# Order of the parts of the inner width in both FFNs: 12, 16, 16 tiles in place of 16, 16, 12

## Chip, core and metric

The kernel runs on one core of one Trainium2 chip. The metric is the device time of one execution in microseconds (us), here the median of three runs. One execution of the kernel before was also taken with the hardware profiler; all rows below are of that one.

## What is computed

Two transformer blocks on one sequence of 256 tokens with 2048 channels, in fp32. Each ends with an FFN of inner width 5632, that is 44 tiles of 128 channels. The first has a causal depthwise convolution of 3 taps between up-projection and gate:

```python
def conv_glu_ffn(h, w_up, cw, cb, w_down):
    u = causal_depthwise_conv(h @ w_up, cw, cb)
    a, gate = jnp.split(u, 2, axis=-1)
    return (jax.nn.silu(gate) * a) @ w_down
```

and the second is `x + (silu(h2 @ w_gate) * (h2 @ w_up)) @ w_down`. After the first FFN come the final norm of block 1 and the input norm of block 2; after the second comes the last norm and the output.

## The kernel before

**Layout.** Channels lie on the 128 partitions, tokens along the free axis (T = 256). x holds 16 tiles. Every weight is split on the chip into a high part (ScalarE, `hi`, L544, the copy itself is L550) and a low part (VectorE, `lo`, L888, the subtraction is L893), both in w_two; activations are likewise split and lie as high and low halves (512 columns) in hp and yp. For each weight tile TensorE runs a pair of matmuls (`unit` L1601): high weight on 512 columns (L1612) and low weight on 256 (L1613).

**Units and slots.** Weights come in units of k tiles by 256 output columns, through R = 4 slots of w_raw and w_two. SyncE issues two DMAs for each unit (L413) as soon as the low part of the slot's earlier unit is done. `hi` of a unit waits until TensorE has used the unit four before it, `lo` waits for `hi`, TensorE for `lo`.

**Phases.** PHASES (L76) lists all weight phases: name, units in a step, steps, output chunks in a step. Each engine has its own program that goes through the phases in this order, written by hand; counters of semaphores are worked out from the table. A part of k tiles of the FFN's inner width gives two phases: up{b}_{p}, k/2 steps of 8 units of 4 tiles, and down{b}_{p}, 4 steps of 8 units of k/4 tiles (a step makes 512 output channels, as two groups of 4 units). So a part of 16 tiles has down units of 4 tiles, one of 12 tiles units of 3 tiles, and `unit_words` (L377) tells both splitting engines how wide a unit is. Each step of an up phase makes two tiles of the gated inner width, called mid; the last of them are finished behind the last matmul of the up phase:

- block 1 (`conv_step`, L736 and L1302): VectorE adds the two halves of the sum out of PSUM (L909, called take), scales (L1010), ScalarE and VectorE do the taps (L731, L1295), ScalarE the sigmoid (L721), VectorE two products (L1317, L1318), ScalarE the high part of mid (L748), VectorE its low part (L1323);
- block 2 (`work`, L1335): the same without taps, low part at L1341.

TensorE's `gemm` (L1634) runs a down phase. Its unit u waits for this many tile pairs of mid:

```python
gemm(f"down{blk}_{p}", m, n, lambda u: (sem("mid"), done + -(-(u + 1) * (n // 4) // 2)))
```

that is 2, 4, 6, 8 of 8 pairs with 16 tiles and 2, 3, 5, 6 of 6 with 12: the fourth unit needs the last pair in both.

**Closing phases.** The parts are added into x on VectorE (`residual`, L1264, with adds at L1268 and L1269). The last part (p == 2, tests at L756 and L1349) isn't a plain stream but `closing` (L601 on ScalarE, L948 on VectorE): while its steps run, the finished tiles of x are squared (L594; with the final gain too at the end of block 1, L597), multiplied by the next norm's gain (L599) and split (L945), with GpSimd adding the squares up (L879). w_out and w_out_2 close in the same way, each with 4 steps; w_out_2 has units of 4 tiles. In the next phase TensorE runs `stats` (L1671): 1-column matmuls that sum squares over channels (L1684), eight for each kind and pair of tiles, behind the next phase's first unit (`opening`, L1696). At the end of block 1 (k == 3) there are two kinds of squares, elsewhere one. In down2_2, which ends the program, `early` (L1656) puts three turns of output (L1588) and the first stats ahead of the very last unit.

Of the kernel before, what the change touches and what calls it, by code (L numbers as in the profile page):

```python
# [47 lines left out]
GC = 256  # L48
# [19 lines left out]
for _name, _cols in (("ident", P), ("flip", P), ("rot", P), ("ones", P), ("cos", T), ("sin", T),  # L68
# [2 lines left out]
    _n += _cols  # L71
NCST = _n

PARTS = [(0, 16), (16, 16), (32, 12)]

PHASES = [("conv", 32, 1, 16), ("kv", 24, 1, 12), ("gates", 2, 1, 1), ("q", 16, 1, 8), ("w_out_conv", 16, 1, 16),  # L76
          ("w_out", 4, 4, 4)]
for _p, (_t, _k) in enumerate(PARTS):
    PHASES += [(f"up1_{_p}", 8, _k // 2, 4), (f"down1_{_p}", 8, 4, 4)]
PHASES += [("latent", 8, 2, 4), ("latent_last", 4, 1, 2), ("kpe", 2, 1, 1), ("mla", 8, 8, 9), ("mla_proj", 8, 4, 4),  # L80
           ("diff", 16, 8, 8), ("diff_proj", 8, 4, 4), ("w_out_2", 8, 4, 4)]
for _p, (_t, _k) in enumerate(PARTS):
    PHASES += [(f"up2_{_p}", 8, _k // 2, 4), (f"down2_{_p}", 8, 4, 4)]
# [47 lines left out]
class Chain:  # L131
# [6 lines left out]
    def link(self, ins):  # L138
        ins.then_inc(self.sem, 1)
        self.k += 1  # L140
        self.wait()
# [59 lines left out]
def program(nc, A, cst_d, out):  # L201
# [5 lines left out]
    with ctx:  # L207
# [169 lines left out]
        def unit_words(ph, j):  # L377
            if ph == "mla" and j < 2:
                return 3 * 384
            return 3 * GC if ph in ("down1_2", "down2_2") else 4 * GC  # L380

        FIRST = {n: m for (n, *_), (m, *_) in zip(PHASES, PHASES[1:])}

# [17 lines left out]
        def _(sp):  # L401
# [75 lines left out]
            def ffn(blk, wa, ca0, wg, cg0, wd):  # L477
                for p, (t0, n) in enumerate(PARTS):
                    ph = f"up{blk}_{p}"
                    with sp.Fori(0, STEPS[ph]) as i:  # L480
                        for g, (w, c) in enumerate(((wa, ca0), (wg, cg0))):
                            col = sp.snap(i * GC + (c + t0 * P))
                            for u in range(4):
                                halves(ph, i, 4 * g + u, w, 4 * u, 4, col)
                    gemm(f"down{blk}_{p}", wd, t0, n, 0)
# [47 lines left out]
        def _(act):  # L533
# [10 lines left out]
            def hi(ph, i, j):  # L544

                s, r = slot_of(ph, j)
                n = unit_words(ph, j)
                act.wait_ge(raw_ready[s], arrived(ph, i, j))
                act.wait_ge(unit_used, i * UPS[ph] + (U0[ph] + j + 1 - R + LEAD))
                nc.scalar.activation(w_hi[:, s, 0:n], w_raw[:, s, 0:n], ACT.Copy).then_inc(hi_ready, 1)  # L550
# [163 lines left out]
            def ffn(blk):  # L714
                for p, (t0, n) in enumerate(PARTS):
                    up = f"up{blk}_{p}"
# [136 lines left out]
        @block.gpsimd  # L853
        def _(pool):
            for s in range(R):
                nc.gpsimd.memset(small[:, 60 + s:61 + s], 0.0).then_inc(lo_ready[s], 1)


            for ph in ("conv", "kv", "gates", "q"):
                for j in range(3 if ph == "conv" else 0, UPS[ph]):  # L860
                    if ph == "conv" and j == 7:
                        pool.wait_ge(sem("bias_row"), 1)
                        pool.dma_start(bias_d, bias_row[0:NQ, :]).then_inc(sem("bias_stored"), 16)
                    if ph == "conv" and j == 10:
                        pool.wait_ge(sem("bias_stored"), 16)
                        pool.dma_start(bias_win, bass.AP(bias_d.tensor, 0, [[1, P], [3 * P, NQ], [1, T]])).then_inc(loaded["bias"], 16)
                    s = slot_of(ph, j)[0]
                    n = unit_words(ph, j)
                    pool.wait_ge(hi_ready, U0[ph] + j + 1)
                    nc.gpsimd.tensor_tensor(w_lo[:, s, 0:n], w_raw[:, s, 0:n], w_hi[:, s, 0:n].bitcast(f32), ALU.subtract)\  # L870
                        .then_inc(lo_ready[s], 1)

            for k in (1, 3, 4, 5):
                for p in range(1, KT // 2 - 1):
                    for src, name, done, nth in ((sq, "squares", "summed", NTH[k]), (sq_g, "squares_g", "summed_g", 0))[:2 if k == 3 else 1]:
                        pool.wait_ge(sem(name), KT // 2 * (nth + 1) + p + 1 if nth or name == "squares" else 2 * p + 2)
                        if p > 1:
                            pool.wait_ge(sem(done), (KT // 2 - 2) * nth + p - 1)
                        nc.gpsimd.tensor_tensor(src[:, 0:2, :], src[:, 0:2, :], src[:, 2 * p:2 * p + 2, :], ALU.add).then_inc(sem(done), 1)  # L879
# [3 lines left out]
        def _(dve):  # L883
# [4 lines left out]
            def lo(ph, i, j):  # L888

                s, r = slot_of(ph, j)  # L890
                n = unit_words(ph, j)
                dve.wait_ge(hi_ready, i * UPS[ph] + (U0[ph] + j + 1))
                v.tensor_tensor(w_lo[:, s, 0:n], w_raw[:, s, 0:n], w_hi[:, s, 0:n].bitcast(f32), ALU.subtract)\  # L893
                    .then_inc(lo_ready[s], 1)
# [380 lines left out]
            def ffn(blk):  # L1275
                if blk == 1:
                    v.memset(ua[:, :, 0:FTAPS - 1], 0.0)
                    link(v.memset(ug[:, :, 0:FTAPS - 1], 0.0))
                for p, (t0, n) in enumerate(PARTS):
                    up, down = f"up{blk}_{p}", f"down{blk}_{p}"  # L1280
# [302 lines left out]
        def _(pe):  # L1583
# [50 lines left out]
            def gemm(ph, rhs, ktiles, operand, between={}):  # L1634

                nu = UPS[ph] // 2
                ku = ktiles // nu
                k = CLOSING.get(ph)

                def step(i, hooks={}):  # L1640
                    for g in range(2):
                        free(ph, i, -2 + 2 * g)
                        for u in range(nu):
                            if (g, u) in hooks:
                                hooks[g, u]()
                            unit(ph, i, nu * g + u, u * ku, ku, GC, (2 * g, 2 * g + 1), rhs, ktiles - 1, operand(u))

                if between:
                    step(0, between)
                whole = STEPS[ph] - (k is not None)  # L1650
                with pe.Fori(1 if between else 0, whole) as i:
                    step(i)
                if k is not None:
                    step(whole, {(1, nu - 1): lambda: early(k)})
# [41 lines left out]
            def opening(k, at):  # L1696

                return {(0, 1): lambda: stats(k, (0, 1, KT - 2, KT - 1)), at: lambda: spread(k)}
# [36 lines left out]
            def normed(k):  # L1735
                if k == 0:
                    return lambda u: (sem("normed_lo"), 2 * u + 2)
                return lambda u: (sem("gained_lo"), KT * NTH[k] + 4 * u + 4)
# [161 lines left out]
            def ffn(blk, k):  # L1900
                h, m = (hp, yp) if blk == 1 else (yp, hp)
                for p, (t0, n) in enumerate(PARTS):
                    gemm(f"up{blk}_{p}", h, KT, normed(k), opening(k, (0, 3)) if p == 0 else {})
# [169 lines left out]
```

## Time and profile before

| | us |
|---|---|
| median of 3 runs | 2911.27 |
| lowest and highest | 2909.68 and 2912.64 |
| the profiled execution, its own time | 2908.53 |
| its span, first to last instruction | 2906.7 |
| TensorE busy in the span | 2852.2 (98%) |
| VectorE, ScalarE, GpSimd busy | 2089.7, 1378.8, 218.8 |
| mean granted TensorE clock | 0.989 |

The span lies inside the time of the same execution; the difference, 1.8 us, is what lies around it. Matmuls are pipelined, so the listed durations of neighbours overlap, and the step from one start to the next is the pace. PEclk is the granted clock as a share of full speed.

### The profile page before, as it was taken

To read this page: it belongs to the slowest core of one execution; us is meant where nothing else is said; L and a number is where in the kernel's file an instruction comes from. 1 tells how busy PE (TensorE), PEld (TensorE's weight loads), DVE (VectorE), ACT (ScalarE), POOL (GpSimd) and SP (SyncE) were. 2 spreads that over 40 slices of the span, in tenths; PEclk is the share of its full clock that TensorE was granted. 3 is DMA by queue.
4 is the path that set the end of the run, shared out by engine and by line. 5 is a ranking of instruction groups with operands and counts; after the bars stand their busy time and mean duration, and the time that the engine had idled before them with its cause. 6 is when DMAs were issued, how large, how long until landed. Compare 5 with 4: busy or idle time off the path is not lost.

```text
span 2906.7 us, 49543 instructions
## 1 busy us (share of the span) xinstructions
PE 2852.2 (98%) x16793; PEld 2489.9 (86%) x16793; DVE 2089.7 (72%) x3289; ACT 1378.8 (47%) x1807; POOL 218.8 (8%) x111
## 2 busy tenths in 40 slices
PE   7998999999999999999999999999999999999998
PEld 6887888888888888888888888888888888888887
DVE  4976777876886687777866777777667766775675
ACT  4324655643554455545443455544455433433434
POOL 4865010000000001100000000000000000000001
PEclk9999999999999999999999999999999999999999
DMA  9645356665655665655555555555555556565654
GB/s 238 181 135 130 95 138 185 185 193 181 187 185 191 185 190 167 178 139 151 153 172 183 169 175 165 179 166 188 185 181 184 189 195 191 176 201 189 188 170 148
DMA packets 605082, 507.34 MB, mean 175 GB/s; under 512 B 90156, under 2 KB 603068, under 8 KB 604604
## 3 DMA queue, kind: packets, MB, share of 16 engines
q1 hardware_dynamic: 604347, 504.00, 57.3%
q0 software_dynamic: 560, 2.12, 0.2%
q8 instruction: 53, 0.87, 0.1%
q14 instruction: 42, 0.34, 0.0%
q10 hardware_dynamic: 80, 0.01, 0.0%
HBM read 503.88 MB, written 2.12 MB: 174 GB/s over the span
## 4 chain that ended last, share of the span: by engine, by line
PE 91%; DVE 4%; ACT 2%; SPq 1%; issue 0%; DMA 0%; POOL 0%; DVEq 0%; ACTq 0%
PE banks L1612 54%; PE banks L1613 28%; PE banks L1625 3%; PE banks L1627 1%; PE banks L1588 1%; ACT hp_f L669 1%; DVE w_two L893 1%; DVE banks L1085 1%; PE banks L1703 0%; PE banks L1958 0%; ACT w_two L550 0%; DVE arena L909 0%; PE banks L2007 0%; PE banks L1684 0%; SPq L397 0%
## 5 line engine op out<-in xcount | busy, mean ns | idle before, releaser
L550 ACT ACTIVATE w_two<-w_raw 128x1024 fp32r<-128x1024 f32 (+2 forms) x960 | 996.8, 1045 | 1161.9 <-PE banks L1613 1073.3
L1612 PE MATMUL banks<-hp,w_two 128*128 128x512 f32 x4160 | 1475.5, 399 | 9.5 <-POOL w_two L870 6.5
L893 DVE TENSOR_TENSOR w_two<-w_raw,w_two 128x1024 fp32r<-128x1024 f32 (+2 forms) x889 | 1071.6, 1217 | 533.1 <-ACT w_two L550 515.6
L1613 PE MATMUL banks<-hp,w_two 128*128 128x256 f32 x4160 | 1167.0, 281 | 0.0
L1612 PE MATMUL banks<-yp,w_two 128*128 128x512 f32 x2752 | 963.8, 395 | 3.9 <-DVE yp L1323 2.6
L1612 PEld LDWEIGHTS banks<-hp,w_two 128*128 128x128 f32 x4160 | 784.7, 189 | 197.8 <-issue 10.3
L1613 PEld LDWEIGHTS banks<-hp,w_two 128*128 128x128 f32 x4160 | 789.3, 190 | 1.4 <-issue 1.0
L1613 PE MATMUL banks<-yp,w_two 128*128 128x256 f32 x2752 | 771.8, 280 | 0.0
L1612 PEld LDWEIGHTS banks<-yp,w_two 128*128 128x128 f32 x2752 | 516.9, 188 | 123.3 <-DVE yp L1323 3.6
L1613 PEld LDWEIGHTS banks<-yp,w_two 128*128 128x128 f32 x2752 | 521.2, 189 | 0.1
L909 DVE TENSOR_REDUCE arena<-banks 128x256 f32<-128x512 f32 (+1 forms) x392 | 251.4, 683 | 80.2 <-PE banks L1613 73.1
L879 POOL TENSOR_TENSOR arena<-arena 128x512 f32<-128x512 f32 x30 | 45.6, 1527 | 2569.5 <-ACT arena L594 2569.5
L870 POOL TENSOR_TENSOR w_two<-w_raw,w_two 128x1024 fp32r<-128x1024 f32 x71 | 171.1, 2423 | 98.3 <-ACT w_two L550 98.3
L1085 DVE SCALAR_TENSOR_TENSOR banks<-arena,vec,banks 128x256 f32<-128x256 f32 x232 | 102.0, 485 | 3.7
L1625 PE MATMUL banks<-w_two,hp 128*128 128x512 f32 x256 | 92.6, 404 | 0.0
L1295 DVE SCALAR_TENSOR_TENSOR arena<-arena,vec 128x256 f32<-128x256 f32 x176 | 77.5, 482 | 17.2 <-ACT arena L731 11.3
L1010 DVE TENSOR_TENSOR arena<-arena,cst 128x512 f32<-128x512 f32 x120 | 82.9, 691 | 3.9
L1612 PE MATMUL banks<-arena_r,w_two 128*128 128x512 f32 x208 | 77.5, 411 | 0.0
L731 ACT ACTIVATE arena<-arena,vec 128x256 f32<-128x256 f32 x88 | 48.2, 595 | 51.3 <-DVE arena L1010 51.3
L1627 PE MATMUL banks<-w_two,hp 128*128 128x256 f32 x256 | 71.9, 281 | 0.0
L721 ACT ACTIVATE arena<-arena 128x512 f32<-128x512 f32 x44 | 27.8, 633 | 80.6 <-DVE arena L1010 61.4
L1268 DVE TENSOR_TENSOR x<-banks,x 128x256 f32<-128x256 f32 (+1 forms) x128 | 53.1, 415 | 15.9 <-PE banks L1613 15.9
(265 smaller groups left out, 1750.4 us busy)
## 6 DMA issues: line engine op xcount, KB each, us to landing
w_raw<-in_w_in SPq DMA_DIRECT2D x480, 256.0 KB, 3.1
w_raw<-in_w_up SPq DMA_DIRECT2D x352, 256.0 KB, 2.9
w_raw<-in_w_ffn_up SPq DMA_DIRECT2D x176, 256.0 KB, 3.7
w_raw<-in_w_ffn_gate SPq DMA_DIRECT2D x176, 256.0 KB, 3.0
w_raw<-in_w_down SPq DMA_DIRECT2D x160, 256.0 KB, 3.0
w_raw<-in_w_ffn_down SPq DMA_DIRECT2D x160, 256.0 KB, 3.0
w_raw<-in_w_out SPq DMA_DIRECT2D x128, 256.0 KB, 3.1
w_raw<-in_w_mla_proj SPq DMA_DIRECT2D x64, 256.0 KB, 3.0
```

The costliest lines, as they stand in the source:

```text
L550: nc.scalar.activation(w_hi[:, s, 0:n], w_raw[:, s, 0:n], ACT.Copy).then_inc(hi_ready, 1)
L870: nc.gpsimd.tensor_tensor(w_lo[:, s, 0:n], w_raw[:, s, 0:n], w_hi[:, s, 0:n].bitcast(f32), ALU.subtract)\
L893: v.tensor_tensor(w_lo[:, s, 0:n], w_raw[:, s, 0:n], w_hi[:, s, 0:n].bitcast(f32), ALU.subtract)\
L909: v.tensor_reduce(dst, pair(b)[0:rows], X, ALU.add).then_inc(chunk_out, 1)
L1010: return v.tensor_tensor(dst, dst, bcast(r_row, 2), ALU.mult)
L1085: ins = v.scalar_tensor_tensor(conv_y[:, t, :] if k == TAPS - 1 else acc, src, w, acc, ALU.mult, ALU.add)
L1268: link(v.tensor_tensor(xt, banks[:, c, 0:T], xt, ALU.add))
L1295: ins = v.scalar_tensor_tensor(dst[:, c, :], buf[:, c, k:k + T], vdyn("ffn_conv_w", at_ch[c] + k * 2 * FT), dst[:, c, :], ALU.mult, ALU.add)
L1612: mm(banks[:, b, :], w_hi[:, s, at:at + P], rhs[:, kt, :], start=kt == kt_first, stop=False)
L1613: ins = mm(banks[:, b, 0:T], w_lo[:, s, at:at + P], rhs[:, kt, 0:T], start=False, stop=kt == kt_last)
L1625: mm(banks[:, b, :].rearrange("p (a n) -> p a n", a=2), rhs[:, kt, b * P:(b + 1) * P], w_two[:, :, s, at], start=kt == 0, stop=False)
L1627: ins = mm(banks[:, b, 0:T], rhs[:, kt, T + b * P:T + (b + 1) * P], w_hi[:, s, at], start=False, stop=kt == kt_last)
```

## The change

The 44 tiles are cut into parts of 12, 16 and 16 tiles. Thereby up{b}_0 has 6 steps and up{b}_2 has 8; down{b}_0 has units of 3 tiles and down{b}_2 of 4. `unit_words` follows. Which phase closes, and all else, is untouched.

```diff
-PARTS = [(0, 16), (16, 16), (32, 12)]
+PARTS = [(0, 12), (12, 16), (28, 16)]
...
         def unit_words(ph, j):
             if ph == "mla" and j < 2:
                 return 3 * 384
-            return 3 * GC if ph in ("down1_2", "down2_2") else 4 * GC
+            return 3 * GC if ph in ("down1_0", "down2_0") else 4 * GC
```

## Rows read from the trace of the kernel before

**Rows 1.** The page: span and busy time of each engine.

```profile
span 2906.7 us, 49543 instructions
...
PE 2852.2 (98%) x16793; PEld 2489.9 (86%) x16793; DVE 2089.7 (72%) x3289; ACT 1378.8 (47%) x1807; POOL 218.8 (8%) x111
```

**Rows 2.** TensorE's waits, whole span: total us, times, longest us.

```profile
PE banks L1684 <- ACT arena L594: 5.0, 3, 2.4
...
PE banks L1612 <- DVE yp L1323: 2.6, 2, 2.3
...
PE banks L1612 <- DVE hp L1341: 1.0, 1, 1.0
```

**Rows 3.** Timeline, TensorE in down1_2: start us, us, instruction; 42 such starts.

```profile
1159.62 0.39 PE L1612 MATMUL banks<-yp,w_two 128*128 128x512 f32 x1
...
1173.83 0.40 PE L1612 MATMUL banks<-yp,w_two 128*128 128x512 f32 x1
```

**Rows 4.** Splits of units of 4 and 3 tiles: busy, mean ns, idle before.

```profile
L550 ACT ACTIVATE w_two<-w_raw 128x1024 fp32r<-128x1024 f32 x880 | 925.8, 1058 | 1106.1 <-PE banks L1613 1018.9 <-PE banks L1627 45.4 <-DMA w_raw<-in_w_in 25.9
L550 ACT ACTIVATE w_two<-w_raw 128x768 fp32r<-128x768 f32 x64 | 53.2, 842 | 52.5 <-PE banks L1613 51.1 <-DMA w_raw<-in_w_ffn_down 1.3
...
L893 DVE TENSOR_TENSOR w_two<-w_raw,w_two 128x1024 fp32r<-128x1024 f32 x809 | 985.9, 1229 | 491.3 <-ACT w_two L550 474.0 <-DVE hp L1341 7.8 <-DVE arena L1492 1.5
...
L893 DVE TENSOR_TENSOR w_two<-w_raw,w_two 128x768 fp32r<-128x768 f32 x64 | 64.7, 1028 | 38.0 <-ACT w_two L550 37.9
```

**Rows 5.** Chain that ended last: the ends of up1_0, up1_2 and up2_2.

```profile
617.30 1.30 DVE arena L909 x2
...
625.10 0.70 DVE yp L1323
...
1111.42 1.30 DVE arena L909 x2
...
1119.21 0.70 DVE yp L1323
...
2823.00 1.21 DVE arena L909 x2
...
2827.54 0.70 DVE hp L1341
```

**Rows 6.** Timeline at the end of down1_2: VectorE, ScalarE, TensorE.

```profile
1181.20 2.52 DVE L893 TENSOR_TENSOR w_two<-w_raw,w_two 128x1024 fp32r<-128x1024 f32 x2 [2.12 <-ACT w_two L550]
...
1184.44 0.41 DVE L1268 TENSOR_TENSOR x<-banks,x 128x256 f32<-128x256 f32 x1
...
1180.13 3.00 ACT L550 ACTIVATE w_two<-w_raw 128x1024 fp32r<-128x1024 f32 x3
1186.13 0.63 ACT L594 ACTIVATE arena<-x 128x512 f32<-128x512 f32 x1 [3.01 <-DVE x L1269]
...
1184.72 1.03 PE L1684 MATMUL banks<-cst,arena 128*128 128x1 f32 x8
1186.81 4.29 PE L1684 MATMUL banks<-cst,arena 128*128 128x1 f32 x24 [1.06 <-ACT arena L594]
```

**Rows 7.** The same at the end of w_out_2.

```profile
2153.24 0.42 DVE L1268 TENSOR_TENSOR x<-banks,x 128x256 f32<-128x256 f32 x1
...
2154.94 0.63 ACT L594 ACTIVATE arena<-x 128x512 f32<-128x512 f32 x1 [0.83 <-DVE x L1269]
...
2155.76 1.93 PE L1684 MATMUL banks<-cst,arena 128*128 128x1 f32 x16
```

**Rows 8.** ScalarE's squares with the final gain: busy, mean ns.

```profile
L597 ACT ACTIVATE arena<-x,vec 128x256 f32<-128x256 f32 x16 | 7.9, 494 | 0.0
```

**Rows 9.** TensorE at the end of w_out.

```profile
439.38 1.05 PE L1684 MATMUL banks<-cst,arena 128*128 128x1 f32 x8 [1.46 <-ACT arena L594]
```

**Rows 10.** Stretches: us, busy of PE, PEld, DVE, ACT, POOL, PEclk, DMA share, GB/s.

```profile
436.00:446.00 10.00, 8.54 (x48) 7.60 (x47) 6.92 (x18) 4.88 (x7) 0.00 (x0) 0.83 0.58 168
1116.00:1123.00 7.00, 4.66 (x19) 3.83 (x18) 5.17 (x8) 3.46 (x5) 0.00 (x0) 0.76 0.24 69
1184.00:1195.00 11.00, 9.94 (x52) 9.19 (x51) 7.06 (x27) 4.86 (x9) 0.00 (x0) 0.69 0.46 142
2152.00:2162.00 10.00, 10.00 (x65) 8.99 (x64) 7.58 (x19) 7.39 (x9) 0.00 (x0) 1.00 0.45 145
2824.00:2832.00 8.00, 7.02 (x41) 5.91 (x40) 6.44 (x10) 3.79 (x5) 0.00 (x0) 1.00 0.31 96
```

## The prediction

> **What bounds the kernel.** I read the page first: TensorE is busy for 2852.2 of 2906.7 us [rows 1], and no other engine is near that. So the change pays or costs only through what TensorE waits for, or the clock it is granted. Next the list of TensorE's waits [rows 2]: of all of them three kinds touch FFN parts. At L1612 it waits 2.6 us in two places for the last mid of block 1, one of 2.3, so the other is 0.3. It waits 1.0 for the last mid of block 2. At L1684 it waits 5.0 in three places for squares behind a closing phase, 2.4 the longest. The reader should see that all of this is 8.6 us, and that the up and down loops themselves show no wait.
>
> **Pace.** In down1_2 42 listed starts of L1612 lie between 1159.62 and 1173.83 [rows 3]: 14.21 / 41 = 0.3466 us for one weight tile (a pair of matmuls). A unit of 4 tiles is 8 pairs, 2.77 us; one of 3 tiles is 6 pairs, 2.08 us. In both kinds the splitting engines are quicker: 1.058 and 1.229 us for 4 tiles, 0.842 and 1.028 for 3 [rows 4]. The short ones' idle time before ScalarE's copies is 52.5 us, of which 51.1 ended with TensorE and 1.3 with a DMA: the loads are in time at the short pace too.
>
> **What the change moves, part by part.**
>
> *Work.* Each block keeps one part of 12 and two of 16: 22 up steps, 12 down steps, 32 short down units and 64 long ones. Matmuls, splits, bytes, DMA issues (two for each unit on SP) and residual adds are the same in number and size, only in another order; GpSimd's adds too. 0 us. The short units' loads, issued on SP, now come ahead of up1_1 and up2_1 instead of the closing. They are hidden by the four slots, as the 1.3 us above shows; without that cover each late load would cost TensorE directly, and the bound is those 1.3 us. The first units of the following up phase are ready at the latest one copy and one subtraction (1.06 + 1.23 = 2.3 us) after the last short unit frees a slot, and three of them (8.3 us) run before the fourth is wanted. 0 us.
>
> *The wait for the last mid.* It moves with the short part. From the take to the low part's end it is 8.50 us at the end of up1_0 (617.30 to 625.10 + 0.70) and 8.49 at that of up1_2 (1111.42 to 1119.21 + 0.70) [rows 5]: the chain doesn't depend on which part it is. TensorE covers it with three down units, 8.32 us for long and 6.24 for short ones. The differences, 0.2 and 2.2, are the measured 0.3 and 2.3. After the change down1_0 waits 0.3 + 2.08 = 2.4 and down1_2 about 2.3 - 2.08 = 0.2: 2.6 together, as before, so 0.0. In block 2 the chain is shorter (2823.00 to 2827.54 + 0.70 = 5.2, after a split that is late [rows 5]); the 1.0 of down2_2 goes to down2_0 and down2_2's falls to 0: 0.0. Bounds: 0.3 either way, the difference between the two block 1 chains as they meet the cover.
>
> *The wait for squares at the end of block 1.* This is where something changes. VectorE should take the last residual as soon as the last down unit ends. In the list of its instructions [rows 6] it waits 2.12 us for ScalarE's splits, does two (2.52 us) and starts the residual at 1184.44. The last down unit ended one unit of 2.77 before the stats at 1184.72 (some 0.1 between), at about 1181.8: the residual is 2.6 us late. ScalarE was late with these splits because the previous pair's squares and gains held it until 1180.13. Four short units (8.3 us) are too little for this round trip between two engines. The square comes at 1186.13, and TensorE has stood for 1.06 us before the 24 stats at 1186.81. w_out_2 closes with long units (11.1 us for four) and is the model for down1_2 after the change [rows 7]: stats at 2155.76, so the last unit ended near 2152.8 and the residual at 2153.24 is only 0.4 late; the square starts at 2154.94, ends at 2155.6, and the 16 stats run with no wait. Down1_2 has two more squares to a pair there (L597, 0.494 each [rows 8]), that is some 1.0 us more on ScalarE before the splits; with 11.1 - 8.3 = 2.8 us more room that still fits. So the 1.06 goes: **-1.1 us**, bounds 0 (ScalarE as late as now) and -1.1. Nothing else is late next: eight stats (1.03 us [rows 6]) run before the squares of the last pair are wanted.
>
> *The end of the program.* The 2.4 us of [rows 2] there is the run from the last matmul through four adds and a square; it starts when the last unit ends, whatever its size. The last unit gets 0.7 us longer, one among others that are shorter. 0 us; there are three turns and eight stats before it, and they have more room now. Also 0.
>
> *The clock.* TensorE runs at 2.4 GHz nearly always. In five stretches [rows 10] it is seen what a wait does. At the end of w_out, with a wait of 1.46 among stats [rows 9], the granted clock is 0.83 over 10 us: 10 x 0.17 = 1.7 us of full speed missing. Around the 2.3 us wait in down1_2 it is 0.76 over 7, again 1.7. At the end of down1_2, where 32 one-column matmuls and the 1.06 wait lie together, 0.69 over 11: 3.4 us missing. At the end of w_out_2 (16 such matmuls, no wait) and around the 1.0 wait of down2_2 it is 1.00: nothing. So a fall to 1.2 GHz costs in pieces of 1.7. The fall around the mid wait moves to down1_0 with the same wait: 0, with -1.7 to +1.7 as bounds. At the end of block 1 the wait goes but the 32 one-column matmuls stay, about 4.1 us of them at 1.03 for eight: nearer to w_out (16 of them and a wait, 3.5 us in all, a fall) than to w_out_2 (1.93 us, none). I take the fall as staying, 0 us, with -3.4 as the other bound.
>
> The Trainium skill (TensorE: Matmul & The Clock Gate, section "The HAM clock gate") says that the full clock is released by activity and that the hardware's look at it is free-running, not tied to the kernel. By that rule the same wait in another place may be met by a fall or not, so it speaks against carrying the falls over one to one, and the sum would be anything from -1.1 - 5.1 = -6.2 to -1.1 + 3.4 = +2.3 us.
>
> **Sum.** 0 + 0.0 - 1.1 + 0 + 0 = -1.1 us. Against the profiled execution's 2908.53 that is 2907.4. That execution lies 2.7 below the median of 2911.27 and 1.2 below the lowest run, so I put the difference on the median: **2910.2 us**.
>
> **Rivals.**
>
> *A, forecast (0.40):* wait gone, falls as before. 2910.2.
>
> *B, the fall at the end of block 1 goes too (0.25).* For it: w_out_2's end at 1.00. Against: twice as many one-column matmuls in a row. It gives 3.4 less the part that was spent standing (1.06 x 0.5 = 0.5), so -1.1 - 2.9 = -4.0: 2907.3. Half of it (one piece of 1.7) lies between A and B.
>
> *C, slower (0.17):* the fall takes hold in the fourth unit of down2_0's first step. There the 1.0 us wait stands alone at 1.00 now; at its new place it may be met by a fall. One piece costs 1.7, two 3.4: -1.1 + 1.7 = +0.6 to -1.1 + 3.4 = +2.3, so about 2912.7. It decides from a fall of over 1.1 us on. Against it: at the same wait nothing fell. (The clock gate page of the Trainium skill, by the section named above, leaves this open.)
>
> *D, nothing to measure anywhere (0.10):* the change doesn't bring what the steps say, because ScalarE with its extra squares is as late as before. 2911.3. For it: the two extra squares. Against it: 2.8 us more room.
>
> *E, faster by over 0.2% (0.04):* that is 5.8 us, about what a measurement of this kernel can tell from no change. It takes the wait, both falls in block 1 (5.1) and some more, as the wait of 2.3 in down1_0 being covered. -6.2 to -8: 2904.2. Every wait of the five places with both falls is 8.6 + 5.1, so more can't come.
>
> *F, slower by over 0.2% (0.04):* something in every step, as late loads or splits, at 0.2 us in each of the 44 up steps of both blocks: 8.8 - 1.1 = +7.7. No row shows such a wait. 2919.0.
>
> **How the numbers follow.** A, B, C and D lie between 2907.3 and 2913.6. With the runs' own spread of 1.5 about the median and the bounds of 0.3 and 1.3 for mid and loads, 2905.3 to 2914.3 leaves out E and F and the tails of B and C. All but E and F are within 5.8 us, so same has 0.90 with the rest of the tails shared: faster 0.06, same 0.89, slower 0.05.
>
> **What the changed profile would show.** TensorE's waits: at L1612 for L1323 again 2.6 in two places, the long one near 580 us instead of 1117 (up1_0 has two steps of 8 x 2.77 us less, so it ends 44 us before 617); for L1341 1.0, now near 2294 (six such steps and three short units behind 2155) instead of 2828; at L1684 two places with 3.9 instead of three with 5.0. The residual at the end of down1_2 starts within 0.5 us of the last matmul, and the 24 stats have no idle before them. TensorE's busy time stays at 2852 give or take 3. Wrong would be: a long wait at down1_2's mid still (the chain is what matters there, not the cover), a wait before 24 stats, or a new wait in up1_1 or up2_1 behind the short units.

## Result, and the profile after

| | before | after |
|---|---|---|
| median of 20 runs, us | 2910.09 | 2917.59 |
| lowest and highest | 2899.86, 2912.99 | 2905.76, 2924.19 |
| ratio, 95% interval | | 1.0024, 1.0016 to 1.0031 |
| the profiled execution | 2908.53 | 2907.34 |
| its span | 2906.7 | 2905.6 |

The change makes the kernel slower by 7.5 us in the median, a little over what can be told from no change. The profiled execution alone says otherwise: it is 1.2 us faster than the one of before, and is the second fastest of its 20. One profile of each kernel, compared by its span, would have led to the wrong sign. What follows explains both. The mean granted clock of every timed execution in this document is 0.987 to 0.994, except for one of e8_before_restart (4214.64 us at 0.619), which is left out of that run's median.

Nearly all that the steps foretold of waits is there. TensorE's waits in the profiled execution of the changed kernel (in all us, times, longest):

```profile
PE banks L1684 <- ACT arena L594: 3.9, 2, 2.4
...
PE banks L1612 <- DVE yp L1323: 2.9, 3, 2.3
...
PE banks L1612 <- DVE hp L1341: 1.0, 1, 1.0
```

The wait at L1341 is still 1.0 [rows 2], L1684 is down from three waits and 5.0 to two and 3.9, and L1323's long one is still 2.3. L1323 has three waits, though, where two and 2.6 in all were foretold: one of 0.3 is new, at 823, at the end of up1_1. In the kernel before, a weight load was 0.4 late there for L1323 too, without a wait of a matmul. The end of down1_2 in three timelines, VectorE, ScalarE, TensorE:

```profile
1167.88 2.70 DVE L893 TENSOR_TENSOR w_two<-w_raw,w_two 128x1024 fp32r<-128x1024 f32 x2 [2.12 <-ACT w_two L550]
...
1171.29 0.42 DVE L1268 TENSOR_TENSOR x<-banks,x 128x256 f32<-128x256 f32 x1
...
1172.99 0.63 ACT L594 ACTIVATE arena<-x 128x512 f32<-128x512 f32 x1 [0.89 <-DVE x L1269]
...
1173.68 4.83 PE L1684 MATMUL banks<-cst,arena 128*128 128x1 f32 x32
```

In [rows 6] the residual was 2.6 us late. Now, by the same working, it is some 0.5 late (the last unit ended one unit of 2.77 and some 0.1 before the stats at 1173.68, at about 1170.8), and all 32 one-column matmuls run without idle. The granted clock still falls there, as forecast: 0.73 over 11 us against 0.69 in [rows 10]. Around the long mid wait, now near 577, it doesn't fall at all (1.00 over 574 to 584, where [rows 10] had 0.76). The view of stretches of the changed kernel, columns as in [rows 10]:

```profile
574.00:584.00 10.00, 7.66 (x45) 6.47 (x44) 8.06 (x12) 5.17 (x7) 0.00 (x0) 1.00 0.45 136
1171.00:1182.00 11.00, 11.00 (x61) 10.22 (x60) 6.51 (x24) 5.92 (x10) 0.00 (x0) 0.73 0.45 138
2280.00:2288.00 8.00, 7.01 (x40) 5.91 (x40) 6.50 (x10) 3.79 (x5) 0.00 (x0) 1.00 0.25 76
640.00:880.00 240.00, 239.74 (x1384) 209.40 (x1383) 185.28 (x246) 116.10 (x135) 0.00 (x0) 1.00 0.61 190
2340.00:2540.00 200.00, 200.00 (x1133) 173.33 (x1132) 138.88 (x160) 79.68 (x80) 0.00 (x0) 1.00 0.59 186
2560.00:2800.00 240.00, 240.00 (x1360) 208.15 (x1359) 157.52 (x183) 93.07 (x92) 0.00 (x0) 1.00 0.59 186
```

**What the steps had not asked.** The last three rows above are stretches of steady up and down work at full clock, with no wait but the 0.3 in the first. The number in brackets is how many matmuls TensorE did. The view of stretches of the kernel before, for the same three and one more of block 1:

```profile
640.00:880.00 240.00, 240.00 (x1361) 208.25 (x1360) 178.27 (x235) 111.72 (x128) 0.00 (x0) 1.00 0.59 185
910.00:1090.00 180.00, 180.00 (x1040) 158.69 (x1039) 129.80 (x170) 81.78 (x92) 0.00 (x0) 1.00 0.61 189
2340.00:2540.00 200.00, 200.00 (x1156) 176.34 (x1155) 130.72 (x155) 78.46 (x77) 0.00 (x0) 1.00 0.59 189
2560.00:2800.00 240.00, 240.00 (x1387) 211.59 (x1386) 159.08 (x186) 95.41 (x94) 0.00 (x0) 1.00 0.59 188
```

In 2560 to 2800 TensorE did 1387 matmuls before and 1360 after, in the same time, at PEclk 1.00, never idle. 240 us / (1387 / 2) is 346 ns for a pair, 240 / (1360 / 2) is 353 ns. Block 1 has it the other way round: in 640 to 880 before had 1361 and after has 1384. So the stream of matmul pairs has two paces, 2% apart. The slow one begins right behind the moved wait. The timeline of TensorE in down2_0 of the changed kernel (start, length, instruction, idle before it):

```profile
2282.37 0.39 PE L1612 MATMUL banks<-hp,w_two 128*128 128x512 f32 x1
...
2282.72 0.39 PE L1612 MATMUL banks<-hp,w_two 128*128 128x512 f32 x1
...
2283.06 0.39 PE L1612 MATMUL banks<-hp,w_two 128*128 128x512 f32 x1
...
2284.56 0.50 PE L1612 MATMUL banks<-hp,w_two 128*128 128x512 f32 x1 [0.99 <-DVE hp L1341]
...
2285.01 0.40 PE L1612 MATMUL banks<-hp,w_two 128*128 128x512 f32 x1
...
2285.38 0.40 PE L1612 MATMUL banks<-hp,w_two 128*128 128x512 f32 x1
...
2285.72 0.40 PE L1612 MATMUL banks<-hp,w_two 128*128 128x512 f32 x1
...
2286.07 0.40 PE L1612 MATMUL banks<-hp,w_two 128*128 128x512 f32 x1
```

Ahead of the wait the starts of L1612 are 0.69 apart for two (2282.37, 2282.72, 2283.06), the quick pace within the rounding of the rows. Behind it the starts are 2285.01, 2285.38, 2285.72, 2286.07: 1.06 for three, 353 ns each, and the rows list 0.40 us where they listed 0.39. It stays so to the last norm's stats at 2887. Before, block 2's only wait for a mid was at 2827, some 60 us ahead of those stats.

A simple measure shows it in every profile: the time from one norm's stats (L1674, the matmul ahead of them) to the next. Block 1's FFN lies between the stats after w_out and those after down1_2, block 2's between those after w_out_2 and the early ones of the last norm. Block 2's two in TensorE's timeline, before and then after:

```profile
2155.62 0.28 PE L1674 MATMUL banks<-small,cst 128*128 128x4 f32 x2
...
2889.06 0.28 PE L1674 MATMUL banks<-small,cst 128*128 128x4 f32 x2
```

```profile
2144.37 0.28 PE L1674 MATMUL banks<-small,cst 128*128 128x4 f32 x2
...
2887.35 0.28 PE L1674 MATMUL banks<-small,cst 128*128 128x4 f32 x2
```

Before: 1184.58 - 436.75 = 747.8 and 2889.06 - 2155.62 = 733.4. After, in the profiled execution: 739.9 and 743.0. Block 2 lost 9.6 us. Block 1 gained 7.9, most of it because it ran at the quick pace in this execution; the repeat below shows that it needn't.

### The profile page after: what moved, and what is told of

It is laid out like the page before. It is cut to its first block, busy times and chain, and to the rows that moved or that the text cites. A ratio compares the mean times of both kernels' runs of the same rounds, so it can differ in the third digit from the quotient of the medians.

```text
span 2905.6 us, 49539 instructions
## 1 busy us (share of the span) xinstructions
PE 2849.6 (98%) x16793; PEld 2480.2 (85%) x16793; DVE 2087.7 (72%) x3289; ACT 1368.8 (47%) x1799; POOL 220.5 (8%) x111
## 4 chain that ended last, share of the span: by engine, by line
PE 92%; DVE 4%; ACT 2%; SPq 1%; issue 0%; DMA 0%; POOL 0%; DVEq 0%; ACTq 0%
PE banks L1612 55%; PE banks L1613 27%; PE banks L1625 3%; PE banks L1627 1%; PE banks L1588 1%; ACT hp_f L669 1%; DVE w_two L893 1%; DVE banks L1085 1%; PE banks L1703 0%; PE banks L1958 0%; DVE arena L909 0%; PE banks L2007 0%; SPq L397 0%; PE banks L1684 0%; DVE hp_f L1187 0%
## 5 line engine op out<-in xcount | busy, mean ns | idle before, releaser
L1612 PE MATMUL banks<-hp,w_two 128*128 128x512 f32 x4160 | 1474.0, 399 | 9.9 <-POOL w_two L870 6.9
L1612 PE MATMUL banks<-yp,w_two 128*128 128x512 f32 x2752 | 966.0, 396 | 4.1 <-DVE yp L1323 2.9
L1612 PEld LDWEIGHTS banks<-hp,w_two 128*128 128x128 f32 x4160 | 783.7, 188 | 200.3 <-issue 10.7
L1612 PEld LDWEIGHTS banks<-yp,w_two 128*128 128x128 f32 x2752 | 516.3, 188 | 128.5 <-DVE yp L1323 3.8
L1612 PE MATMUL banks<-arena_r,w_two 128*128 128x512 f32 x208 | 77.1, 410 | 0.0
```

What stands on the lines that cost most here:

```text
L1612: mm(banks[:, b, :], w_hi[:, s, at:at + P], rhs[:, kt, :], start=kt == kt_first, stop=False)
```

## The experiments

The first four runs ask only where the loss is. From e5 on there are two theories. **P**: a disturbance of TensorE's stream (a wait, an odd burst) decides which of two paces follows, and the pace stays until the next one; so the moved 1.0 us wait costs 10 us by what lies behind it. **L**: short units early, or their loads, cost the time by themselves. Each was timed beside the kernel before, e1 to e12 with 11 or 12 executions, but e8 and e12 with 7 and e11 with 6. The last two columns are the two FFNs' times in the one profiled execution, as just defined.

| run | median us | ratio, 95% interval | profiled us | block 1 | block 2 |
|---|---|---|---|---|---|
| before (first profile) | | 1 | 2908.53 | 747.8 | 733.4 |
| after (first profile) | 2917.59 | 1.0024, 1.0016 to 1.0031 | 2907.34 | 739.9 | 743.0 |
| e1_again | 2910.21 | 1.0013, 1.0000 to 1.0027 | 2918.18 | 750.3 | 743.0 |
| e2_block1 | 2904.99 | 0.9990, 0.9977 to 1.0002 | 2911.37 | 752.0 | 733.4 |
| e3_block2 | 2917.71 | 1.0025, 1.0011 to 1.0038 | 2918.33 | 749.2 | 743.0 |
| e4_middle | 2911.64 | 1.0008, 0.9996 to 1.0020 | 2911.64 | 750.1 | 737.8 |
| e5_wait_alone | 2916.84 | 1.0028, 1.0010 to 1.0046 | 2911.09 | 745.7 | 744.0 |
| e6_block2_restart | 2910.80 | 1.0015, 0.9999 to 1.0032 | 2907.25 | 750.6 | 732.6 |
| e7_changed_restart | 2908.31 | 1.0003, 0.9988 to 1.0019 | 2916.14 | 748.8 | 740.9 |
| e8_before_restart | 2920.83 | 1.0046, 1.0029 to 1.0064 | 2926.57 | 750.2 | 745.3 |
| e9_block2_no_wait | 2906.90 | 0.9985, 0.9973 to 0.9998 | 2908.51 | 747.0 | 730.4 |
| e10_changed_finer | 2904.30 | 0.9984, 0.9972 to 0.9997 | 2892.92 | 740.0 | 730.4 |
| e11_before_finer | 2897.42 | 0.9958, 0.9942 to 0.9974 | 2899.38 | 742.5 | 731.1 |
| e12_block2_finer | 2897.62 | 0.9963, 0.9950 to 0.9976 | 2897.18 | 740.9 | 730.4 |

The kernel before had a median of 2908.49 beside e1 to e4, 2909.73 beside e5 to e8, 2909.21 beside e9 to e12. The ratio is taken over all executions and differs from the quotient of the two medians by up to 0.0011 (e6), so differences of a us or two between medians say little.

### Where is it: e1 to e4

The parts became a table by block, here for e3:

```diff
-PARTS = [(0, 16), (16, 16), (32, 12)]
+PARTS = {1: [(0, 16), (16, 16), (32, 12)], 2: [(0, 12), (12, 16), (28, 16)]}
```

e2 has the other block changed, e4 the parts 16, 12, 16 in both, e1 is the changed kernel as it stands.

> The changed kernel once more. Known so far: its profiled execution took 2907.34 us, 1.2 less than that of before and as the steps had it, but its median of 20 is 2917.59. Theory A (the loss is in the program and shows in most executions): median again 6 to 9 us above before, and the profile, if it is of a typical execution, shows TensorE waiting about 8 us somewhere that it doesn't in before. Theory B (the loss belongs to the time or chip of the first comparison): within 2 us of before.

> 12, 16, 16 in block 1 only, 16, 12... kept as 16, 16, 12 in block 2. Theory A1 (the loss is in block 1, loads or splits late around the short units or around the new place of the phases): +6 to +9 us against before. Theory A2 (in block 2): -1 us, from the gone wait for squares. Theory A3 (half in each): +3 us.

> 12, 16, 16 in block 2 only, block 1 as before. Theory A1 (loss in block 1): 0 us. Theory A2 (loss in block 2): +7 to +9 us. Theory A3 (half in each): +4 us.

> 16, 12, 16 in both blocks. If the loss comes from a short part that is followed by an up phase, or from long units in the closing, it is the same as with 12, 16, 16: +7 us. If it comes from where up_0 and the first down phase lie in time, it is gone: -1 us.

e1's profiled execution is a long one, 2918.18, and has the same longer waits as the first profile: 2.3 for L1323, 1.0 for L1341; the two of 0.3 are not in it. Between the two executions of one program lie 10.8 us, and 10.4 of them in block 1, 750.3 against 739.9. Its median of 11 is only 1.7 above before, against 7.5 in the first 20: the medians of a kernel with two paces depend much on which executions were drawn. This repeat alone would lie inside the forecast's range. e2 and e3 settle the place: block 1's change alone gives -3.5 us (its interval reaches just past 1), block 2's alone +9.2, and block 2's time is 743.0 in each of after, e1 and e3, to the tenth. e4 lies between: its wait comes one part later (at about 2560), and block 2 takes 737.8. So what block 2 pays shrinks with what is left of the program behind the wait: 4.4 us with some 330 us left, 9.6 with some 600. This alone doesn't exclude L, by which a short part might cost less the later it comes.

### Is it the wait: e5

```diff
-gemm(f"down{blk}_{p}", m, n, lambda u: (sem("mid"), done + -(-(u + 1) * (n // 4) // 2)))
+gemm(f"down{blk}_{p}", m, n, lambda u: (sem("mid"), done + (n // 2 if blk == 2 and p == 0 and u > 1 else -(-(u + 1) * (n // 4) // 2))))
```

> Parts as in the kernel before; only in the first step of down2_0 units 2 and 3 ask for the last mid pair, so that TensorE waits there (5.2 us of chain behind the last up unit and 2.1 for the split ahead of it, less two long units of 5.5: about 1.7 us). Theory P (a wait sets the pace of the matmul stream that follows; after a wait at L1341 the pair of matmuls takes 353 in place of 347 ns until the next event): +1.7 from the wait and 0.0067 us for each of the 1560 pairs from 2290 to 2825, 10.4: together +10 to +12 us, and the profile shows 353 from there. Rival L (short units or their place cost the time, by loads or splits): +1.7 us only, at 347.

No part is moved here, and +7.1 us is measured (ratio 1.0028). TensorE's wait for mid in 2270 to 2360 of its profile, and then its stretches in block 2:

```profile
PE banks L1612 <- DVE hp L1341: 2.2, 1, 2.2
```

```profile
2340.00:2540.00 200.00, 200.00 (x1134) 173.34 (x1133) 128.01 (x152) 76.99 (x76) 0.00 (x0) 1.00 0.58 183
2560.00:2800.00 240.00, 240.00 (x1361) 208.25 (x1360) 156.92 (x183) 92.49 (x92) 0.00 (x0) 1.00 0.59 186
```

There are 2.2 us of wait near 2330 and then 1134 and 1361 matmuls in the stretches where before has 1156 and 1387: 353 ns. Block 2 takes 744.0, 10.6 more, of which the wait is 2.2. The forecast of 10 to 12 holds for block 2, and the median is below it. One reason can be read in the profile: the later wait for mid, 0.9 us at 2831, turned the stream back to the quick pace (233 matmuls in 2840 to 2880, where before has 229). L would have given 1.7, and the interval of the ratio is +2.9 to +13.4 us. So a wait without any short unit ahead of it costs what the changed order costs.

### Does a burst put the pace back: e6 to e8

```diff
+def again():
+    for c in range(4):
+        mm(banks[:, 7, c:c + 1], ident, ones[:, 0:1], start=True, stop=True)
...
-gemm(f"down{blk}_{p}", m, n, lambda u: (...))
+gemm(f"down{blk}_{p}", m, n, lambda u: (...), {(1, 0): again})
```

in down2_0 alone (e6, on top of e3), or in all six down phases (e7, e8). (1, 0) puts the burst ahead of the fifth unit of a phase's first step, so behind the unit that waits.

> Block 2 alone changed, as in the run that lost 9 us, and in down2_0 four one-column matmuls (eight instructions, about 1 us) behind the fifth unit's start, after the wait. Theory P, with such a burst putting the pace back (the stats ahead of up2_0 did so in all six profiles): +1 us against before, 9 less than without, profile at 347 from there. Theory P without that: +10 us. Rival L: +10 us.

> The changed kernel with that burst in the first step of all six down phases (about 6 us of work more). Theory P with the burst putting the pace back: 6 more, 10 less in block 2, about 5 less in block 1: 2909, 8 below the changed kernel. Rival L: 6 above the changed kernel.

> The kernel before with the same six bursts. Theory P: +6 of work, -5 for block 1's stretch at 353 ns (625 to 894) and -1 behind down2_2: 0 against before. Rival L: +6.

e6's timeline of TensorE around the wait and the burst (L1903) in down2_0:

```profile
2294.82 0.50 PE L1612 MATMUL banks<-hp,w_two 128*128 128x512 f32 x1 [0.98 <-DVE hp L1341]
...
2295.27 0.40 PE L1612 MATMUL banks<-hp,w_two 128*128 128x512 f32 x1
...
2296.69 0.40 PE L1612 MATMUL banks<-hp,w_two 128*128 128x512 f32 x1
...
2297.05 0.95 PE L1903 MATMUL banks<-cst 128*128 128x1 f32 x8
...
2298.64 0.39 PE L1612 MATMUL banks<-hp,w_two 128*128 128x512 f32 x1
...
2300.02 0.39 PE L1612 MATMUL banks<-hp,w_two 128*128 128x512 f32 x1
```

From 2295.27 to 2296.69 the pace is 355 (1.42 for four), from 2298.64 on 345 (1.38 for four). The burst did turn it, and block 2 takes 732.6 in this execution. But e8 refutes that a burst puts the pace *back*. Its down2_0 has long units and no wait, and the stream was at 347 ahead of the same burst. Its timeline of TensorE:

```profile
2348.71 0.39 PE L1612 MATMUL banks<-hp,w_two 128*128 128x512 f32 x1
...
2349.75 0.39 PE L1612 MATMUL banks<-hp,w_two 128*128 128x512 f32 x1
...
2350.10 0.95 PE L1903 MATMUL banks<-cst 128*128 128x1 f32 x8
...
2351.69 0.40 PE L1612 MATMUL banks<-hp,w_two 128*128 128x512 f32 x1
...
2355.23 0.40 PE L1612 MATMUL banks<-hp,w_two 128*128 128x512 f32 x1
```

Behind it 2351.69 to 2355.23 is 3.54 for ten, 354 ns, and it stays at the slow pace through block 2, which takes 745.3. The kernel is 11.1 us slower than before, where P had 0 and the bursts' own work alone is some 6. e7 shows both outcomes in one profile. Its stretches behind the burst of down2_0 and behind that of down2_1, near 2545, where no wait is listed:

```profile
2340.00:2540.00 200.00, 200.00 (x1156) 176.34 (x1155) 139.60 (x163) 80.68 (x82) 0.00 (x0) 1.00 0.62 194
2560.00:2800.00 240.00, 240.00 (x1360) 208.11 (x1360) 158.67 (x186) 93.09 (x92) 0.00 (x0) 1.00 0.59 184
```

So a burst, like a wait, decides the pace anew and not always the good one. e6 and e7 came out 1.1 above and 1.4 below before, about as theory P with the burst putting the pace back had it, but with spreads of 21.6 and 20.6 us and by a premise that e8 refutes.

### The stream left alone: e9 to e12

Two edits. The first lets VectorE add up the last PSUM halves of an up phase of block 2 ahead of the split of the fourth down unit (e9). The second (with the first in e10 to e12) asks for the last mid pair only at the last two tiles of the fourth unit.

```diff
 def stream(ph, out_a, out_b, work=None, pre_next=True, low=0):
...
                     elif pre_next:
-                        first(FIRST[ph])
+                        lows(FIRST[ph], 0, 0, 3 if ph[:3] == "up2" else min(4, UPS[FIRST[ph]]))
                     used(ph, i, UPS[ph])
                     out_b(i)
+                    if last and ph[:3] == "up2":
+                        lows(FIRST[ph], 0, 3, 4)
...
 def unit(ph, i, j, k0, ku, cols, where, rhs, kt_last, operand=None, kt_first=0, last=None):
...
                 for k in range(ku):
                     kt = k0 + k
+                    if last and k == ku - 2:
+                        pe.wait_ge(*last)
...
-                    gemm(f"down{blk}_{p}", m, n, lambda u: (sem("mid"), done + -(-(u + 1) * (n // 4) // 2)))
+                    gemm(f"down{blk}_{p}", m, n, lambda u: (sem("mid"), done + -(-(u + 1) * (n // 4) // 2) - (u == 3)),
+                         last=(sem("mid"), done + n // 2))
```

> Block 2 alone changed to 12, 16, 16, and the 1.0 us wait ahead of down2_0's fourth unit taken away: in the last up step of block 2 VectorE adds up its PSUM halves (out_b) before the split of the fourth down unit, not behind it, so mid is finished about 1.7 us earlier (0.96 of split and what it waited for). Theory P (each disturbance of the matmul stream sets its pace anew, an undisturbed stream keeps 347 ns): no wait in block 2, 347 ns from 2157 to the end, median 0 to 2 us below before and 9 below the run with block 2 changed. Rival L (short units early cost time by themselves): +8 as in that run.

> The changed kernel with that move, and with the last mid pair asked for only at the fourth unit's last two tiles (1.4 us more cover for long units, 0.7 for short). Theory P: block 2 undisturbed at 347; block 1 waits 1.6 once in down1_0 at 580, and from there 347 or 353 until the closing (540 us, 10 us apart): 2900 to 2911, median about 2905. Rival L: as the changed kernel, 2917.

> The kernel before (16, 16, 12) with both edits. Theory P: no wait from 447 to 1117, so the stretch at 353 ns from 625 to 894 (770 pairs, 5.1 us) is gone as well as the one behind down2_2 (1 us): 4 to 7 us below before, and a narrower spread. Rival L: 0 to -1.5, the waits alone.

> Block 1 as before, block 2 12, 16, 16, both edits. Theory P: same as the kernel before with both edits within 1.5 us, since without waits the place of the short part in block 2 decides nothing. Rival L: 8 above it.

e9 is the same order of parts as e3 without the wait, and it is 2.3 us *below* before where e3 was 9.2 above. No wait at L1341's place is left in its list, and its block 2 is at the quick pace throughout, as its stretches show:

```profile
2160.00:2270.00 110.00, 110.00 (x636) 96.96 (x636) 75.82 (x91) 56.44 (x56) 0.00 (x0) 1.00 0.58 186
2340.00:2540.00 200.00, 200.00 (x1156) 176.41 (x1155) 141.31 (x165) 80.97 (x82) 0.00 (x0) 1.00 0.61 193
2560.00:2800.00 240.00, 240.00 (x1387) 211.65 (x1386) 160.28 (x187) 95.20 (x94) 0.00 (x0) 1.00 0.60 189
```

e11 and e12 differ only in the order of parts in block 2, as before and e3 do, and they are 0.2 us apart (before and e3: 9.2), with 6 and 7 executions. Without waits in block 2 its order decides nothing that can be measured here. e10 keeps one wait of 1.6 in down1_0, with 540 us behind it, and spreads from 2892.92 to 2909.72; its median, 2904.30, is where P had it, and L had 2917. e11 has its one at the end of block 1 and spreads from 2891.94 to 2899.38. e11's one wait for L1323 (L1325 there) in the whole span, and block 1's stretches:

```profile
PE banks L1616 <- DVE yp L1325: 1.6, 1, 1.6
```

```profile
640.00:880.00 240.00, 240.00 (x1386) 209.80 (x1385) 181.53 (x241) 114.07 (x131) 0.00 (x0) 1.00 0.61 189
910.00:1090.00 180.00, 180.00 (x1040) 157.31 (x1040) 130.98 (x174) 82.89 (x94) 0.00 (x0) 1.00 0.61 188
```

1386 and 1040 matmuls, where before has 1361 and 1040: block 1's slow stretch is gone. e11 is 11.8 us faster than the kernel before (0.9958, 0.9942 to 0.9974), by more than the 4 to 7 expected. Part of the reason may be that I had taken before's loss from one profile, in which block 1 turned back to 347 ns at the end of up1_1, at 894, where a weight load was 0.4 us late and no wait of a matmul is listed. In e6's profile, with the same block 1, it stays at 353 from 630 to the closing (1360 matmuls in 640 to 880 and 1021 in 910 to 1090, 750.6 us). The kernel before may pay that in some of its executions; its one profile doesn't show it, and how the 11.8 divide is open.

## Why the prediction was wrong

- **The pace** is the step that failed. "14.21 / 41 = 0.3466 us for one weight tile" was read in one stretch of block 1 and taken for the whole program. The first profile showed otherwise: its 640 to 880 has 1361 matmuls, 353 ns a pair. One more line in the view of stretches would have shown two paces in a kernel that the prediction held to be bound by exactly that stream.
- **The wait for the last mid** was moved rightly (long ones of 2.3 and 1.0, where 2.4 and 1.0 were foretold; in block 2 at 2284, where 2294 was; and a third one of 0.3 in block 1 that was not foretold) and priced wrongly: "0.0" in both blocks. In block 2 the true price is the 1.0 us, which cancels, and 607 us behind it (2285 to the end of the last unit) at 353 instead of 347 ns: 607 / 0.3533 x 0.0067 = 11.5, less some 1.1 for the 60 us that ran at 353 behind down2_2 before. 10.4; the profiles have 9.6. That the first profile took 2907.34, and the forecast for it was 2907.4, is luck: block 2's loss of 9.6 met block 1's gain of 7.9, neither of which the sum has, and the other stretches were 2.9 shorter. I had looked at what a wait costs while it lasts and what it does to the clock, not at what the stream looks like behind it.
- **The wait for squares** went as forecast: 1.06 to 0, residual 0.5 late, stats with no idle. That is real in all profiles of the changed block 1, and e2's -3.5 is of this sign; how much of the 3.5 is this wait, and how much the pace that block 1's executions drew, these runs don't separate.
- **The clock** was within its bounds: 3.4 us of full speed missing at the end of block 1 became 11 x 0.27 = 3.0, the 1.7 at the mid wait became 0 in the profiled execution. No rival on the clock carried the loss.
- **Loads, splits, DMA, GpSimd at 0 us**: for block 2 confirmed by e12 against e11; no pair of runs isolates them in block 1.
- **Rival F** had the sign and size (slower by more than 0.2%) with the wrong mechanism and 0.04; its sentence "no row shows such a wait" was true, because the time is lost in busy rows. **Rival C** had the right place, the fourth unit of down2_0's first step, and the wrong price: it asked for the granted clock, which stays 1.00 from 2280 to 2288.
- **The range** went by the sum and the clock alone; its spread of 1.5 us came from three runs. The 20 of before span 13 us, which points to something that differs between executions; the six of e11 span 7.4.

## What to carry to other kernels

Price a wait on the bounding engine by what follows it too: after it, count the instructions in equal stretches with no wait, before and behind, and compare. Where the stream can fall into a slower rhythm, a short wait early in a long undisturbed run can cost far more than the same one at its end (here 1.0 us at 2284 against 1.0 us at 2827), so close the small waits (finer operands, the urgent sum ahead of the patient split) before reordering work. And judge a change of a few us by the medians of many executions: here two profiles of one program lay 10.8 us apart.

## What the runs showed of the hardware

- A steady stream of fp32 matmul pairs (512 and 256 columns, each with its weight load) has at least two rhythms at the full granted clock: starts every 347 ns, or a pattern of three pairs in 1.060 us, 353 ns each. Both run for hundreds of us through units, steps and phases. The Trainium skill (TensorE: Matmul & The Clock Gate, section "Wait — 56ns, not 53.3ns?") gives N / 2.4 GHz and about 2.5 ns from one matmul to the next, for N columns at full clock, by which an estimate for such a pair is 325 ns; both measured rhythms are slower.
- The rhythm can change at a wait (of 0.3, 0.9, 1.0, 2.2 us), at a weight load that was 0.4 late, or at a burst of eight one-column instructions, in either direction. The same program draws differently in different executions: the 2.3 us wait in down1_0 of the changed kernel was followed by 1384 matmuls in 640 to 880 in the first profile and by 1358 in e1. The stats ahead of up2_0 were followed by 347 ns in all 14 profiles. In block 2 the outcome was steady: wherever a wait for L1341 of 1.0 us (2.2 in e5) met the quick stream, in nine profiles, the slow one followed. What in the timing of a wait picks the rhythm is open; no run here varies it alone.
- The granted clock (1.00 in both), the DMA share (0.59 in both in 2560 to 2800) and the lists of waits don't tell the rhythms apart; counts and start times do. The listed length of L1612 rose from 0.39 to 0.40 us at the wait in down2_0 but is no sure sign: near 830 in the changed kernel, at the quick pace, it is 0.40 and 0.39 in turn.
